# A second token tensor's rows go from 1088 to 1152 bytes, with another start and another place for k = 15

## What is computed

```
h = concatenate([meta_b, x], axis=1)          # 16 meta tokens + 256 tokens
u = rms_norm(h, g_pre_mix[l])
proj = u @ w_in[l]
z_pool, v_conv, g_conv, gate_a, gate_b = jnp.split(proj, splits, axis=-1)
y_a = causal_multiscale_pool(z_pool, ...) @ w_pool_out[l]
y_b = conformer_conv(v_conv, g_conv, ...) @ w_conv_out[l]
m = jax.nn.sigmoid(gate_a) * y_a + jax.nn.sigmoid(gate_b) * y_b
```

## Time and profile before

| | |
|---|---|
| median of 3 runs | 2025.81 us (2025.7 to 2026.65) |
| the profiled execution, its own time | 2026.39 us |
| its span, first to last instruction | 2024.6 us |
| PE busy | 2013.1 us, 99% of the span, 10488 matmuls |
| PE weight loads (PEld) | 1715.0 us, 85% |
| DVE busy | 1513.4 us, 75% |
| ACT busy | 1016.1 us, 50% |
| DMA | 389.33 MB, mean 192 GB/s |
| granted clock of TensorE | 0.999 in the mean |

### The profile page before, as it was taken

One profiled execution on the slowest core, in us unless ns is written; L12 is line 12 of the kernel. 1 busy time (PEld: TensorE's weight loads), 2 busy tenths in 40 slices (PEclk: granted clock), 3 DMA queues, 4 the chain that ended last, 5 costly groups with the idle time before them and its releaser, 6 DMA issues.

```text
span 2024.6 us, 28913 instructions
## 1 busy us (share of the span) xinstructions
PE 2013.1 (99%) x10488; PEld 1715.0 (85%) x10488; DVE 1513.4 (75%) x2051; ACT 1016.1 (50%) x1329; POOL 82.9 (4%) x91
## 2 busy tenths in 40 slices
PE   9999999999999999999999999999999999999998
PEld 7888898888888888999888888888888888888886
DVE  6766766566756655578999856588987997898896
ACT  6645444555544544433444644454563464365353
POOL 0000102001002000002000000000000000000001
PEclk9999999999999999999999999999999999999999
DMA  9687655655667656555666566655576467467563
GB/s 348 198 202 186 177 157 172 190 175 174 179 203 243 192 190 185 175 176 159 189 195 198 178 218 185 192 173 160 190 238 195 156 208 226 146 208 235 178 209 134
DMA packets 265477, 389.33 MB, mean 192 GB/s; under 512 B 12504, under 2 KB 147032, under 8 KB 264571
## 3 DMA queue, kind: packets, MB, share of 16 engines
q1 hardware_dynamic: 262587, 377.19, 61.1%
q0 software_dynamic: 2624, 10.54, 1.9%
q10 hardware_dynamic: 144, 0.01, 0.0%
HBM read 385.02 MB, written 2.54 MB: 191 GB/s over the span
## 4 chain that ended last, share of the span: by engine, by line
PE 98%; SPq 1%; DMA 1%; DVE 0%; ACT 0%; issue 0%; DVEq 0%
PE acc L705 18%; PE acc L682 17%; PE acc L683 17%; PE acc L684 17%; PE acc L703 10%; PE acc L696 2%; PE acc L695 2%; PE acc L697 2%; PE aux L734 1%; PE aux L736 1%; PE aux L735 1%; PE acc L701 1%; PE acc L734 1%; PE acc L736 1%; PE acc L735 1%; PE aux L1638 1%
## 5 line engine op out<-in xcount | busy, mean ns | idle before, releaser
L536 DVE TENSOR_TENSOR low_rows<-stage_rows,high_rows 128x1024 fp32r<-128x1024 f32 x494 | 585.8, 1202 | 267.1 <-ACT high_rows L521 260.4
L521 ACT ACTIVATE high_rows<-stage_rows 128x1024 fp32r<-128x1024 f32 x494 | 506.6, 1034 | 516.1 <-PE acc L684 441.4
L521 ACT ACTIVATE w_high<-stage 128x1024 fp32r<-128x1024 f32 (+1 forms) x264 | 276.1, 1047 | 395.2 <-PE acc L705 292.9
L536 DVE TENSOR_TENSOR w_low<-stage,w_high 128x1024 fp32r<-128x1024 f32 (+1 forms) x264 | 319.9, 1220 | 173.9 <-ACT w_high L521 169.5
L705 PE MATMUL acc<-u,w_high 128*128 128x512 f32 x900 | 248.0, 394 | 0.0
L705 PE MATMUL acc<-hT,w_high 128*128 128x512 f32 x645 | 177.5, 394 | 0.0
L705 PEld LDWEIGHTS acc<-u,w_high 128*128 128x128 f32 x900 | 152.9, 189 | 19.1
L703 PEld LDWEIGHTS acc<-u,w_low 128*128 128x128 f32 x960 | 146.8, 188 | 20.5
L703 PE MATMUL acc<-u,w_low 128*128 128x256 f32 x960 | 152.4, 281 | 0.0
L682 PE MATMUL acc<-high_rows,hT 128*128 128x512 f32 x384 | 151.8, 395 | 0.0
L684 PE MATMUL acc<-high_rows,hT 128*128 128x512 f32 x384 | 149.6, 390 | 0.0
(11 more groups left out here) (451 smaller groups left out, 3690.1 us busy)
## 6 DMA issues: line engine op xcount, KB each, us to landing
stage_rows<-in_w_in SPq DMA_DIRECT2D x160, 512.0 KB, 3.7
stage<-in_w_in SPq DMA_DIRECT2D x136, 512.0 KB, 3.6
stage_rows<-in_w_down SPq DMA_DIRECT2D x128, 512.0 KB, 4.4
stage<-in_w_up SPq DMA_DIRECT2D x120, 512.0 KB, 4.5
stage_rows<-in_w_o SPq DMA_DIRECT2D x64, 512.0 KB, 4.1
stage_rows<-in_w_pool_out SPq DMA_DIRECT2D x16, 512.0 KB, 3.9
stage_rows<-in_w_conv_out SPq DMA_DIRECT2D x16, 512.0 KB, 4.4
stage_rows<-in_w_mem_kv SPq DMA_DIRECT2D x14, 512.0 KB, 10.9
```

The costliest lines, as they stand in the source:

```text
L521: act.activation(high[:, pr, k_from:kt, 0:p.cols], src[:, slot, k_from:kt, 0:p.cols], ACT.Copy).then_inc(high_done, 1)
L536: dve.tensor_tensor(low[:, pr, k_from:kt, 0:p.cols], src[:, slot, k_from:kt, 0:p.cols], high[:, pr, k_from:kt, 0:p.cols].bitcast(F32), ALU ...
```

## The change

The tensor is now `u_wide`, 16 x 2 rows of 288 columns (`WIDE`), 1152 bytes, of which the last 16 columns are not used, from Z + 62 KB. It ends at Z + 98 KB. `Wide` stands for uT and maps group k to place (k + 1) mod 16: k = 15 takes the first place, Z + 62 to Z + 64.25 KB, where merged_pair's last rows are while w_o runs. So `beside_wo` writes the meta columns of k = 0 to 14, and those of k = 15 are written in `residual_low` before unit 7's low rows, after u_high has come to 16. PE streams columns 0 to 271 of a row.

```diff
--- before.py
+++ after.py
@@ -32,6 +32,7 @@
 T = 256
 META = 16
 TM = T + META
+WIDE = TM + 16
 A_HEADS, B_HEADS, C_HEADS = 6, 12, 4
 IDX_HEADS, IDX_DIM, B_DIM = 16, 64, 64
 TOPK = min(256, T // 4)
@@ -256,7 +257,7 @@
         meta_in = at("meta_in", Z + 68, [META, D])
         meta_t = at("meta_t", Z + 76, [P, KT, META])
         h_rows = at("h_rows", Z, [P, 2, D])
-        uT = at("uT", Z + 64.0625, [P, KT, 2, TM], F32R)
+        u_wide = at("u_wide", Z + 62, [P, KT, 2, WIDE], F32R)
         rstd_bc = at("rstd_bc", 72.25, [P, TM])
         diag = at("diag", 73.375, [P, 2, P])
         meta_diag = at("meta_diag", 74.375, [META, META])
@@ -428,6 +429,14 @@
         def by_rows(w, col0, slabs, lhs, ready=None):
             return Part(w, col0, slabs, None, ready, cols=ROW, stride=ROW, rows=lhs)
 
+        class Wide:
+
+
+            def __getitem__(self, at):
+                _, k, half, cols = at
+                return u_wide[:, (k + 1) % KT, half, cols]
+
+        uT = Wide()
         u_rows = Tokens(uT, META)
         jobs = {}
         order = [
@@ -445,7 +454,7 @@
         order.append(("w_o", Job(4, [by_rows(A["w_o"], 0, [2] * 8, merged_pair, ("merged_ready", 0))], 2)))
 
         def wide_part(col0, stride):
-            return Part(A["w_in_2"], col0, full, lambda k: (uT[:, k, 0, :], uT[:, k, 1, :]), ("pair_ready", 16), width=TM, stride=stride)
+            return Part(A["w_in_2"], col0, full, lambda k: (uT[:, k, 0, 0:TM], uT[:, k, 1, 0:TM]), ("pair_ready", 16), width=TM, stride=stride)
 
         order += [
             ("glu_in", Job(4, [wide_part(POOL_W, GROUP), wide_part(POOL_W + CONV_W, GROUP)], 2)),
@@ -2262,6 +2271,11 @@
                 r = RESIDUAL_AT[name].get(n if name == "glu_in" else n - 1)
                 if r is not None:
                     for q in (2 * r, 2 * r + 1):
+                        if q == 7:
+                            dve.wait_ge(s("u_high"), 16)
+                            v = tmp[:, 0, (KT - 1) * META:KT * META]
+                            link(dve.tensor_copy(uT[:, KT - 1, 0, 0:META], v))
+                            link(dve.tensor_tensor(uT[:, KT - 1, 1, 0:META], v, uT[:, KT - 1, 0, 0:META].bitcast(F32), ALU.subtract))
                         low_scaled(uT, q, 2 + q % 2, META, "g_pre_mix_2", "u_high", 0)
 
             def beside_wo(n):
@@ -2274,8 +2288,9 @@
                     v = tmp[:, 0, 0:KT * META].rearrange("p (k t) -> p k t", k=KT)
                     link(dve.tensor_tensor(v, meta_t[:],
                                            params[:, g0:g0 + KT].unsqueeze(2).to_broadcast([P, KT, META]), ALU.mult))
-                    link(dve.tensor_copy(uT[:, :, 0, 0:META], v))
-                    dve.tensor_tensor(uT[:, :, 1, 0:META], v, uT[:, :, 0, 0:META].bitcast(F32), ALU.subtract).then_inc(s("meta_ready"), 1)
+                    first = v[:, 0:KT - 1, :]
+                    link(dve.tensor_copy(u_wide[:, 1:KT, 0, 0:META], first))
+                    dve.tensor_tensor(u_wide[:, 1:KT, 1, 0:META], first, u_wide[:, 1:KT, 0, 0:META].bitcast(F32), ALU.subtract).then_inc(s("meta_ready"), 1)
                 residual_low("w_o", n)
                 if n == 31:
                     dve.wait_ge(s("h1_squared"), 8)
```

## The result

The change made the kernel slower: 2029.28 us in the median of 22 runs (2028.5 to 2030.4) against 2026.42 us for the kernel before in 22 runs beside it (2025.7 to 2027.93), ratio 1.0014, 95% interval [1.0008, 1.002]. That is 2.9 us more, where 1.2 us less was forecast, and above the range's upper end of 2028.6. The profiled execution took 2030.07 us with a span of 2028.3 us.

The account below looks back on a forecast made before the run. PE was taken as the bound, by the distance between matmul starts. Held tokens gave -1.2 us and all other terms 0: 2025.2 from the profiled 2026.39, or 2024.6 us against the median, range 2021.1 to 2028.6.

Parts of the forecast that it names:

- Wide stage: 1152 matmuls streaming token rows past held weights: no change from aligned rows, bounds -0.6 to +2.5 us.
- Held tokens: 768 matmuls holding tokens: half the placement penalty goes, 1.5 ns each, -1.2 us.
- The penalty of 3.0 ns against y_pair: Held-token matmuls: 3.0 ns a step more than with well placed y_pair, 2.3 us over 768 matmuls.
- the extra is on all three lines: Held-token lines L682 to L684: 395, 393, 393 ns against 390 with y_pair, so the offset by itself is not the price.
- DVE's late meta columns: Two 128x16 DVE instructions before the last two L2188: about 0.35 us, hidden from PE, taken 0.
- Early meta, DMAs, ACT, POOL, SP: Early meta instructions shrink from 16 to 15 groups off PE's path, the others issue the same instructions: 0.
- Placement does nothing: Both stages: the extra 3.0 ns comes from neighbours in time, not the address; 2025.8 us, chance 0.22.
- The held offset is the price: Held tokens: all three loads 64 off now pay, 6.0 ns more on 768 matmuls, +4.6 us, 2030.4; chance 0.07.
- Aligned streams in a dearer pattern: Wide stage: streams fall into the streamed weights' dearer pattern, +2.5 us, 2027.1 to 2028.3; chance 0.13.

Follow-up runs that it names:

- e16: Changed kernel with 1280-byte rows from Z + 57.9375 KB, k = 13 to 15 late, the pool's window moved, m in four pieces; 2023.23 us, ratio 0.9982.
- e17: e16 with the token tensor alone 128 bytes further (Z + 58.0625 KB); 2030.42 us.
- e18: e16 with the token tensor alone 64 bytes further (Z + 58 KB); 2029.85 us.
- e3: Changed kernel with 1088-byte rows and k = 0 to 14 at their old addresses, only k = 15 in front with late meta columns; 2027.48 us, ratio 1.0002.
- e5: Kernel before with m_pair, the held operand of w_o_2, 128 bytes later and nothing else; 2028.27 us in one run.
- e1: Changed kernel with the start of u_wide 64 bytes later, held slices on multiples of 128 and streamed rows 64 off; 2028.99 us, ratio 1.0011.
- e13: Kernel before with the whole arena 64 bytes later, so no distance between two addresses changes; 2026.25 us beside 2026.5.

## Why the prediction was wrong

The terms added up to -1.2 us and the two stages moved by +2.8: of the 4.0 us between them the held stage has 2.5 and the wide stage 1.5.

1. **Wide stage, taken 0 with -0.6 to +2.5: +1.5 us.** Inside its bounds, and 0.4 to 1.5 of it is the placement's, but the reason for 0 failed: e16 and e17 differ by 3.3 ns a step by the tensor's start alone. That L695 was as long as L696 and L697 was read as "no effect of the offset". The duration of a line doesn't show whose price it is: in the changed kernel's held stage the low slices, at the cheap distance 192, have the longest line (L693, 397 ns), and in e18, with all held slices alike, starts still lie 231 and 235 to 236 ns apart in turn. The test also ran on the grid of 128. Why the mixed rows of the changed kernel take 126.0 ns stays open.
2. **Held tokens, -1.2 us: measured +1.3 us. This is the step that failed**: "After the change all k repeat one pattern. I take half of the penalty". The penalty of 3.0 ns against y_pair was real, and e16 collected it (226.7 ns). But the change did not move towards y_pair. y_pair is at 0 modulo 256; the change gave up the odd k's high slices at 0 (two of their three) and put all high slices at 64, where m_pair pays most (6.4 ns). By the plain mean of m_pair's prices 230.2 becomes 232.0 ns, with the limits of that mean told above. One pattern for all k is no gain in itself: e18 has one and takes 233.3 ns. That "the extra is on all three lines" was taken to mean that the offset isn't the price; it shows nothing, as in point 1.
3. **DVE's late meta columns, 0.35 us hidden: right.** 0.17 + 0.17 us in the trace, 0.4 us of delay in DVE's queue, the fourth slab no later, e3 alone at 1.0002 [0.9993, 1.0011].
4. **Early meta, DMAs, ACT, POOL, SP, 0: right as far as shown.** Chain and clock are unchanged, and e3, which has all of the change but the placement, costs nothing.

The rivals. *Placement does nothing* fell: e18 and e16 differ by 64 bytes in one tensor's start and by 6.6 us. The rule that the rival drew from the Trainium skill (SBUF — State Buffer, "Who interferes with whom"), independent read ports for the moving operand and for weight loads and a PE that never waits, does not hold for PE's step here: the same matmuls take 226.7 or 233.3 ns by the placement of one tensor alone, and the measurement decides. What in the chip makes the difference no run shows. *The held offset is the price* had the direction and nearly the place (a slice at 64 is dear), with a wrong rule: by it slices on the multiple of 128 would have been cheap, and e5 and e1 show 5.4 ns more, and 233.4 ns. Its 6.0 ns per matmul were meant on top of the step before; the held stage gave 1.65, since the slices before paid already. (Its threshold was off too: if one load of three pays before and three pay after, 5.3 ns more means 7.9 ns a load, not 8.3.) *Aligned streams in a dearer pattern* had the wide stage's direction (126.0; it said 126.6), and its upper end of 2028.3 lacked only the held stage's loss. No rival joined the two, since each was argued from one stage; so the range ended at 2028.6.

What the rows of before left open: 230.1 and 229.8 ns with slices on and off the grid of 128 in every k fit a period of 256 as well as one of 128. By the single slices even and odd k would differ under a period of 256, yet the trace has 1.377 us for both, so these rows could not tell the two apart. A kernel that shifts one held tensor by 128 bytes does.

## What to carry to other kernels

Where PE is the bound and each matmul brings its own weight load, look at how the held operand's start stands to the streamed one's modulo 256 bytes. Row lengths that are a multiple of 256 make all k stand alike, and held 512-column products were cheapest at distance 0. Since the rule for the 272-column stream is another one and the cause isn't known, shift the one tensor by 64 bytes up to three times and read the step from the timeline. Judge an offset by the common step of a long run, never by which line's duration is longer. An alignment to 64 or 128 bytes is no goal in itself: here e18, with its streamed rows on the multiple, took 2029.85 us, and e16, 64 bytes before it, 2023.23.

## What the runs showed of the hardware

- A matmul of 128x512 in fp32r, with a weight load of its own and all held slices alike, takes a step of 226.7 ns at distance 0 (e16), 233.3 at 64 (e18) and 232.4 at 128 (e17). With m_pair 32 costs as much as 64, 192 costs 2.1 ns and 256 costs 0.1 above 0. A shift of the whole arena by 64 bytes (e13) changes nothing.
- A wide step of 272 columns takes 123.4, 125.4 or 126.7 ns with all streamed rows at 192, 0 or 64.
- Slices at unlike distances can cost more than their mean: 231.1 for 0, 0, 192, where the mean is 227.7, and 233.4 for 128, 128, 0, where it is 230.6.
- One placement of the token tensor shows two steps in the wide stage, 124.5 ns in six kernels and 125.6 in two, each held for 1080 matmuls.
